# A two-layer hybrid trunk: the last expert in two halves of its inner columns, and the end of the last layer in another form

## The reference

```python
w = aff[top 2 experts of the best group]; w = w / sum(w)
for e in range(16):
    gate, up = split(tok @ w_gu[e])            # 1024 -> 2 x 512
    out = out + comb[:, e:e+1] * ((silu(gate) * up) @ w_down[e])   # 512 -> 1024
x = layer_norm(ALPHA * x + g2 * out, ln_g[l, 1], ln_b[l, 1])
```

## Time and profile before

| | |
|---|---|
| Time, median of 3 runs | 1354.54 us (1351.35 to 1356.68) |
| The profiled execution's own time | 1352.85 us |
| Its span | 1351.0 us |
| Mean granted TensorE clock | 0.966 |
| PE / DVE / ACT / POOL busy | 1244.5 / 1038.0 / 769.2 / 276.5 us |

### The profile page before, as it was taken

The page is one execution under the profiler, slowest core; times in us unless marked ns, Lnnn a source line. Parts: engine busy times, 40 slices in busy tenths (PEclk is TensorE's granted clock), DMA queues, the critical chain, the costliest instruction groups (busy, mean ns, idle before and its releaser), DMA issues.

```text
span 1351.0 us, 17986 instructions
## 1 busy us (share of the span) xinstructions
PE 1244.5 (92%) x6571; PEld 964.2 (71%) x6572; DVE 1038.0 (77%) x1162; ACT 769.2 (57%) x1032; POOL 276.5 (20%) x321
## 2 busy tenths in 40 slices
PE   4999999699999999899998999999959999999975
PEld 4876677477777777569866777857747777777752
DVE  6787768789999998667737666643778999989857
ACT  3523224377777777554635565575347777777750
POOL 0112222100000000337005555444120000000020
PEclk9999999699999999899988999999969999999988
DMA  9887973599999999914943333215359999999961
GB/s 356 304 276 282 339 269 110 205 365 406 392 373 408 386 400 374 371 36 155 234 122 94 110 98 106 94 64 195 127 195 365 385 402 386 391 392 393 373 240 62
DMA packets 111950, 359.22 MB, mean 266 GB/s; under 512 B 8048, under 2 KB 16476, under 8 KB 111850
## 3 DMA queue, kind: packets, MB, share of 16 engines
q1 hardware_dynamic: 89992, 282.10, 57.1%
q0 software_dynamic: 17296, 60.38, 12.5%
q10 hardware_dynamic: 4594, 15.84, 2.9%
HBM read 329.94 MB, written 25.21 MB: 263 GB/s over the span
## 4 chain that ended last, share of the span: by engine, by line
PE 53%; DVE 15%; issue 11%; ACT 10%; DMA 5%; POOL 3%; SPq 1%; ACTq 1%; DVEq 0%; POOLq 0%
PE bank L237 13%; PE bank L238 12%; PE bank L239 12%; ACT w_hi L1399 4%; DMA ada<-in_ada_w_dram 3%; PE bank L2298 2%; DVE acc L468 2%; PE bank L2280 2%; POOL prob L2520 2%; DVE hh L1501 2%; ACT xe_hi L1345 2%; PE bank L1438 2%; PE bank L1328 1%; PE bank L2268 1%; DVE w_lo L232 1%
## 5 line engine op out<-in xcount | busy, mean ns | idle before, releaser
L1405 DVE TENSOR_TENSOR w_lo<-raw,w_hi 128x2048 fp32r<-128x2048 f32 x189 | 433.6, 2298 | 51.8 <-ACT w_hi L1399 49.8
L1399 ACT ACTIVATE w_hi<-raw 128x2048 fp32r<-128x2048 f32 x189 | 362.6, 1918 | 80.7 <-PE bank L239 78.4
L237 PE MATMUL bank<-w_lo,xe_hi 128*128 128x512 f32 x512 | 212.3, 415 | 1.3 <-DVE xe_lo L1360 1.1
L238 PE MATMUL bank<-w_hi,xe_lo 128*128 128x512 f32 x512 | 204.4, 399 | 0.0
L239 PE MATMUL bank<-w_hi,xe_hi 128*128 128x512 f32 x512 | 204.1, 399 | 0.0
L227 ACT ACTIVATE w_hi<-raw 128x2048 fp32r<-128x2048 f32 x37 | 70.6, 1910 | 112.5 <-PE bank L239 84.4
L1317 POOL DMA_INDIRECT xg<-scratch_u,tok x32 | 31.4, 980 | 481.9 <-PE bank L1328 456.8
L237 PE MATMUL bank<-u_lo,w_hi 128*128 128x512 f32 x288 | 119.3, 414 | 9.0 <-DVE q L2185 4.2
L2520 POOL TENSOR_SCALAR prob<-prob,rsum,gates 128x512 f32<-128x512 f32 (+3 forms) x128 | 108.2, 858 | 91.0 <-DVE rsum L2488 91.0
L237 PEld LDWEIGHTS bank<-w_lo,xe_hi 128*128 128x128 f32 x512 | 97.5, 190 | 30.7 <-issue 8.5
L238 PE MATMUL bank<-u_hi,w_lo 128*128 128x512 f32 x288 | 115.6, 401 | 0.0
(11 more groups left out here) (332 smaller groups left out, 2279.9 us busy)
## 6 DMA issues: line engine op xcount, KB each, us to landing
raw<-in_w_gu_dram SPq DMA_DIRECT2D x128, 1024.0 KB, 7.4
raw<-in_w_down_dram SPq DMA_DIRECT2D x64, 1024.0 KB, 6.5
ada<-in_ada_w_dram POOLq DMA_DIRECT2D x48, 512.0 KB, 6.6
ada<-in_ada_w_dram SPq DMA_DIRECT2D x32, 512.0 KB, 3.8
scratch_y<-ye ACTq DMA_DIRECT2D x30, 512.0 KB, 7.2
raw<-in_conv_w_in_dram SPq DMA_DIRECT2D x12, 1024.0 KB, 14.3
mod_w<-in_ada_w_dram SPq DMA_DIRECT2D x8, 1024.0 KB, 14.0
raw<-in_w_kv_dram SPq DMA_DIRECT2D x6, 1024.0 KB, 6.8
```

What stands on the lines that cost most here:

```text
L237: nc.tensor.matmul(o, lh, rl, start=start, stop=False)
L238: nc.tensor.matmul(o, ll, rh, start=False, stop=False)
L1399: nc.scalar.activation(w_hi[:, hslot, :], raw[:, slot, :], ACT.Copy).then_inc(hi_done, 1)
L1405: nc.vector.tensor_tensor(w_lo[:, slot, :], raw[:, slot, :], w_hi[:, hslot, :].bitcast(F32), ALU.subtract).then_inc(lo_done, 1)
```

## The change

The last expert of both layers is computed in two halves of its 512 inner columns. `gate_up_halves` reads the weight block as two strips of 256 columns (gate and up of one half) and fills bank 2 + f with both, for the last two gate and up blocks and for the two that run under expert 14; sg, hh, the transposes (banks 6 and 7), ht_hi and ht_lo come once per half. On VectorE the lo part of the last down block moves behind ht_lo. The silu of the first half waits for a semaphore from the first half of the last gate and up block, the second for the whole block.

In layer 1 ScalarE scales the first gathered row of each tile by its weight, VectorE adds the second one with its weight and multiplies by the gate row (`far_gate_dve`), and VectorE also makes ye, with the gate row in it. `end_pe` sums ALPHA * xt (through a diagonal matrix), the gathered sum (through the identity) and the last expert's part in two banks per tile, other banks for each tile. `norm_end_dve` takes statistics and the first half of the normalization straight from PSUM. For tiles 0 to 2 ScalarE scales and GpSimd adds row 1; for tile 3 VectorE does both in one operation, behind a wait for tile 2. The diagonal matrices are one in place of eight. Left out of the diff: semaphore counts for these steps, and two waits inside the branch that is skipped.

```diff
-    def norm_last_dve(dve, s, i):
-
-        if i == 0:
-            dve.wait_ge(*moes[s.l].pre_in.at(16 * 12))
+    def norm_end_dve(dve, s, i, banks):
+        for h in range(2):
+            nc.vector.bn_stats(ln_stat[:, i, 6 * h:6 * h + 6], bank[banks[h]][:]).then_inc(dve_step, 1)
+            dve_n[0] += 1
+        dve.wait_ge(dve_step, dve_n[0])
+        nc.vector.bn_aggr(ln_mv[:, i, 0:2], ln_stat[:, i, :].rearrange("p (a b) -> p a b", b=6)
+                          ).then_inc(s.stat.sem, 1)
         dve.wait_ge(*s.stat.at(i + 1))
-        nc.vector.scalar_tensor_tensor(out=xt[:, i, :], in0=xt[:, i, :], scalar=ln_mv[:, i, 0:1],
-                                       in1=end_row(0), op0=ALU.subtract, op1=ALU.mult).then_inc(s.gain.sem, 1)
+        for h in range(2):
+            c_ = slice(h * BANK, (h + 1) * BANK)
+            m = nc.vector.scalar_tensor_tensor(out=xt[:, i, c_], in0=bank[banks[h]][:], scalar=ln_mv[:, i, 0:1],
+                                               in1=end_row(0)[:, c_], op0=ALU.subtract, op1=ALU.mult)
+        m.then_inc(s.gain.sem, 1)
         dve.wait_ge(*s.root.at(i + 1))
         nc.vector.reciprocal(ln_mv[:, i, 3:4], ln_mv[:, i, 2:3]).then_inc(s.coef.sem, 1)
-        dve.wait_ge(*s.gain.at(i + 1))
-        dve.wait_ge(*s.coef.at(i + 1))
-        nc.vector.scalar_tensor_tensor(out=xt[:, i, :], in0=xt[:, i, :], scalar=ln_mv[:, i, 3:4],
-                                       in1=end_row(1), op0=ALU.mult, op1=ALU.add).then_inc(s.done.sem, 1)
+        if i == TT - 1:
+            dve.wait_ge(*s.gain.at(i + 1))
+            dve.wait_ge(*s.coef.at(i + 1))
+            dve.wait_ge(*s.done.at(i))
+            nc.vector.scalar_tensor_tensor(out=xt[:, i, :], in0=xt[:, i, :], scalar=ln_mv[:, i, 3:4],
+                                           in1=end_row(1), op0=ALU.mult, op1=ALU.add).then_inc(s.done.sem, 1)
...
+    def norm_scale_act(act, s, i):
+        act.wait_ge(*s.gain.at(i + 1))
+        act.wait_ge(*s.coef.at(i + 1))
+        nc.scalar.activation(xt[:, i, :], xt[:, i, :], ACT.Copy, scale=ln_mv[:, i, 3:4]).then_inc(s.norm.sem, 1)
+    def norm_shift_pool(pool, s, i):
+        pool.wait_ge(*s.norm.at(i + 1))
+        nc.gpsimd.tensor_tensor(xt[:, i, :], xt[:, i, :], end_row(1), ALU.add).then_inc(s.done.sem, 1)
...
+    def half_cols(ap, f):
+        return ap.rearrange("p (h f n) -> p f h n", h=2, f=2)[:, f, :, :]
+    def gate_up_halves(pe, s, pair, p, i, j, last_block=False):
+        b, slot, _, hslot = step_block(s, pair, p, i)
+        pe.wait_ge(lo_done, b + 1)
+        for f in range(2):
+            for kk in range(2):
+                k = 2 * j + kk
+                c_ = slice(kk * D, (kk + 1) * D)
+                m = mm3(bank[2 + f][:].rearrange("p (h n) -> p h n", h=2), xe_hi[:, 1, k, :], xe_lo[:, 1, k, :],
+                        half_cols(w_hi[:, hslot, c_], f), half_cols(w_lo[:, slot, c_], f), start=(k == 0),
+                        stop=(k == KD - 1))
+            if last_block and f == 0:
+                m.then_inc(s.xg_turned.sem, 1)
+        m.then_inc(blk_used, 1)
...
+        ahead_of_last = isinstance(pair, int) and e == NE - 2
+        if last:
+            gate_up_halves(pe, s, pair, p, 0, 2)
+            gate_up_halves(pe, s, pair, p, 1, 3, last_block=True)
+        else:
+            gate_up(pe, s, pair, p, 0, p, 2)
             rows_pe(pe, s, pair + p, q)
-        gate_up(pe, s, pair, p, 1, p, 3)
-        if not last:
+            gate_up(pe, s, pair, p, 1, p, 3)
             pe.wait_ge(*s.xe_lo_made.at(e + 2))
             after(pe, s.h_made, e)
-            gate_up(pe, s, pair, p, 2, q, 0)
+            if ahead_of_last:
+                gate_up_halves(pe, s, pair, p, 2, 0)
+            else:
+                gate_up(pe, s, pair, p, 2, q, 0)
...
         for k in range(4):
-            m = nc.tensor.transpose(bank[6][:, k * P:(k + 1) * P], hh[:, k * P:(k + 1) * P], ident[:])
+            if last and k == 2:
+                m.then_inc(s.h_turned.sem, 1)
+                pe.wait_ge(*s.h_made.at(e + 2))
+            m = nc.tensor.transpose(bank[6 + (k // 2 if last else 0)][:, k * P:(k + 1) * P],
+                                    hh[:, k * P:(k + 1) * P], ident[:])
         m.then_inc(s.h_turned.sem, 1)
-        if not last:
+        if ahead_of_last:
+            gate_up_halves(pe, s, pair, p, 3, 1)
+        elif not last:
             gate_up(pe, s, pair, p, 3, q, 1)
...
+            if last and j == 1:
+                pe.wait_ge(*s.ht_lo_made.at(e + 2))
...
-        act.wait_ge(blk_used, s.b0 + EBLK * e + 4)
-        after(act, s.h_made, e)
-        nc.scalar.activation(sg[:], bank[2 * p][:], ACT.Silu).then_inc(s.sg_made.sem, 1)
-        if not last:
+        if last:
+            act.wait_ge(*s.h_made.at(e))
+            for f in range(2):
+                if f == 0:
+                    act.wait_ge(*s.xg_turned.at(NE + 1))
+                else:
+                    act.wait_ge(blk_used, s.b0 + EBLK * e + 4)
+                nc.scalar.activation(sg[:, f * HALF:(f + 1) * HALF], bank[2 + f][:, 0:HALF], ACT.Silu
+                                     ).then_inc(s.sg_made.sem, 1)
+            for f in range(2):
+                act.wait_ge(*s.h_turned.at(e + f + 1))
+                nc.scalar.activation(ht_hi[:, 2 * f:2 * f + 2, :], bank[6 + f][:, f * HALF:(f + 1) * HALF]
+                                     .rearrange("p (k t) -> p k t", k=2), ACT.Copy).then_inc(s.ht_hi_made.sem, 1)
+        else:
+            act.wait_ge(blk_used, s.b0 + EBLK * e + 4)
+            after(act, s.h_made, e)
+            nc.scalar.activation(sg[:], bank[2 * p][:], ACT.Silu).then_inc(s.sg_made.sem, 1)
             step_hi(act, s, pair, p, 4)
-        act.wait_ge(*s.h_turned.at(e + 1))
...
+            if s.l == 1:
+                m = nc.scalar.activation(dg[:, 0, :], ident[:], ACT.Copy, scale=ALPHA)
+            for j in range(2 * TT if s.l == 0 else 0):
                 m = nc.scalar.activation(dg[:, j, :], ident[:], ACT.Copy, scale=w_far[:, j % 2, j // 2:j // 2 + 1])
...
+        if last and s.l == 1:
+            for i in range(TT):
+                act.wait_ge(*s.yg_in[i].at(32))
+                nc.scalar.activation(yg[2 * i][:], yg[2 * i][:], ACT.Copy, scale=w_far[:, 0, i:i + 1]
+                                     ).then_inc(s.far_scaled.sem, 1)
+            return
...
-        step_lo(dve, s, pair, p, 3)
-        dve.wait_ge(*s.sg_made.at(e + 1))
-        after(dve, s.h_turned, e)
-        nc.vector.tensor_tensor(hh[:], sg[:], bank[2 * p + 1][:], ALU.mult).then_inc(s.h_made.sem, 1)
-        if not last:
+        if last:
+            dve.wait_ge(*s.h_turned.at(e))
+            for f in range(2):
+                c_ = slice(f * HALF, (f + 1) * HALF)
+                dve.wait_ge(*s.sg_made.at(e + f + 1))
+                nc.vector.tensor_tensor(hh[:, c_], sg[:, c_], bank[2 + f][:, HALF:FF], ALU.mult
+                                        ).then_inc(s.h_made.sem, 1)
+            for f in range(2):
+                dve.wait_ge(*s.ht_hi_made.at(e + f + 1))
+                nc.vector.tensor_tensor(ht_lo[:, 2 * f:2 * f + 2, :], bank[6 + f][:, f * HALF:(f + 1) * HALF]
+                                        .rearrange("p (k t) -> p k t", k=2),
+                                        ht_hi[:, 2 * f:2 * f + 2, :].bitcast(F32), ALU.subtract
+                                        ).then_inc(s.ht_lo_made.sem, 1)
+            step_lo(dve, s, pair, p, 3)
+        else:
+            step_lo(dve, s, pair, p, 3)
+            dve.wait_ge(*s.sg_made.at(e + 1))
+            after(dve, s.h_turned, e)
+            nc.vector.tensor_tensor(hh[:], sg[:], bank[2 * p + 1][:], ALU.mult).then_inc(s.h_made.sem, 1)
             step_lo(dve, s, pair, p, 4)
-        dve.wait_ge(*s.ht_hi_made.at(e + 1))
...
+        else:
+            for i in range(TT - 1):
+                norm_shift_pool(pool, s.ln, i)
...
+            if s.l == 1 and i < TT - 1:
+                norm_scale_act(act, s.ln, i)
...
+        if s.l == 1:
+            far_gate_dve(dve, s, 0)
+            dve.wait_ge(blk_used, s.b0 + EBLK * NE)
+            after(dve, s.y_out[1], 16 * (PAIRS - 1))
+            for h in range(2):
+                c_ = slice(h * BANK, (h + 1) * BANK)
+                m = nc.vector.tensor_tensor(ye[:, 1, c_], bank[4 + h][:], row(s.ln.gate)[:, c_], ALU.mult)
+            m.then_inc(s.y_made.sem, 1)
+            for i in range(1, TT):
+                far_gate_dve(dve, s, i)
         over_dve(dve, s)
+        if s.l == 1:
+            for i in range(TT):
+                dve.wait_ge(*s.comb.at(i + 1))
+                norm_end_dve(dve, s.ln, i, END_BANKS[i])
+                if i == TT - 1:
...
+    END_BANKS = ((0, 1), (2, 3), (6, 7), (4, 5))
+    def far_gate_dve(dve, s, i):
+        if i == 0:
+            wait_row(dve, s.ln.gate)
+        dve.wait_ge(*s.far_scaled.at(i + 1))
+        far = yg[2 * i]
```

(56 more changed lines are left out.)

12 lines of the change are left out of this document (7 added, 5 removed).

## The result

| | before | changed |
|---|---|---|
| Median of 5 runs | 1353.28 us (1351.35 to 1356.68) | 1343.65 us (1341.32 to 1345.97) |
| Ratio | | 0.9934 [0.9917, 0.9951], so -8.9 us |
| Profiled execution / its span | 1352.85 / 1351.0 us | 1345.97 / 1344.2 us |
| Mean granted clock | 0.966 | 0.968 |

The kernel became faster by 0.5 to 0.8%, inside the range of the prediction, but by 8.9 us and not by 13.3. The profile taken is that of the slowest of the five changed runs, 6.8 us shorter in its span. The chain of waits, with which the earlier trace rows began, breaks off after three pieces in this trace, so I read the stretches from the timelines.

A forecast was written before the change was run, and what follows sets the result against it. TensorE holds 53% of the chain of waits, but VectorE bounds layer 1's end. Layer 1's 11.3 us plus layer 0's 2.0 make 13.3, taking the 1354.54 us median to 1341; range 1334.5 to 1347.

The forecast's parts named there:

- The halves and the clock: Last expert, layer 1: down starts 2.4 us earlier and full clock saves 1.6 us, together 4.0 us.
- rival (c): Gate and up products fed slower in strips of 256; at half rate 9 us slower, 1363; chance 0.04.
- (d): Last expert's halves do not overlap, handovers cost what they save; only 7.3 us gained, 1347; chance 0.08.
- Layer 1's end: VectorE finishes 4.5 us behind TensorE instead of 11.8; with the earlier down products, 11.3 us gained.
- with it the 3.2 us at a clock of 0.52: Layer 1's combination: the low-clock stretch after TensorE's 3.10 us pause stays as long as before.
- an earlier tile 0: Layer 0's combination starts 2.0 us sooner, limited by the second gather; bounds 4.2 gained to 1 lost.
- the hold-up: Layer 0: w_lo runs over the first gather, so the second lands near 563.4; without it 4.2 us gained.
- a loss of 1: Layer 0's lower bound: block loads starting some 5 us sooner push the gathers, losing 1 us.
- The tail: From VectorE's last operation, 1348.00, to the span's end, 1351.0, brought by the last output transfer; no change in the sum.
- (a): Layer 1's end is paced by VectorE or gathers, late gathers held 2 to 4 us; near 1344; chance 0.22.
- (b): Layer 0 gives nothing and the low clock stays in the down products; 9.7 us gained, 1345; chance 0.16.

The follow-up runs named there:

- e3: Changed kernel with layer 0's last expert whole as before, halves only in layer 1; ratio to before 0.9933.
- e6: Changed kernel with VectorE doing the last operation of all four tiles, without ScalarE's scaling and GpSimd's sums there; ratio to before 0.9954.
- e8: Changed kernel with GpSimd adding the row for tiles 0 and 1 only, VectorE ending tiles 2 and 3; ratio to before 0.9926.
- e10: e6 plus a GpSimd memset of one unread column after VectorE's last operation; one run, no ratio, span 1346.0 us.
- e4: Changed kernel with SyncE issuing layer 0's next two weight loads only after tile 1's gathers have landed; ratio to before 0.9956.
- e11: e9 without VectorE's wait in layer 0 for tile 1's gathered rows; ratio to before 0.9912, median 1339.8 us.
- again: The changed kernel itself, unaltered, timed and profiled a second time; ratio to before 0.9913.
- e2: Changed kernel without halves in either layer, keeping only the new end of layer 1; ratio to before 0.9956.
- e5: e4 with VectorE's next two w_lo in layer 0 also waiting for tile 1's gathers; ratio to before 0.9953.
- e7: Changed kernel with unread TensorE products added: two in layer 1 ahead of the skip, five in layer 0 behind it; ratio to before 0.9963.
- e9: Changed kernel with e5's waits, e8's two tiles, and unread products ahead of the skip (three in layer 0, two in layer 1); ratio to before 0.9914.

## Why the prediction was right, and where not

**The halves and the clock: right.** Down starts 2.83 us earlier (forecast 2.4) and takes 5.88 us at clock 1.00 in all kernels with halves (forecast 5.7); in layer 1 TensorE gained 4.24, forecast 4.0. Gate and up products in strips are still 0.23 us apart, so rival (c) falls; the handovers overlap, so (d) falls.

**Layer 1's end: right in kind, 1.0 us too much.** From TensorE's last product to VectorE's last operation are 4.46 us, forecast 4.52. The GpSimd sum takes 2.34 us, forecast 2.3, though it runs beside VectorE's statistics. The whole stretch gave 10.3 of 11.3. What lacks is the step "with it the 3.2 us at a clock of 0.52": tile 0 ran 6 us at 0.50. In e3 to e6 and e8 the stretch is 37.6 to 37.9, a gain of 11.5 to 11.8. Both profiles of the changed kernel have the long low clock (tile 0 done at 19.1), and the six others with halves, the new end and nothing added in the pause (e3 to e6, e8, e10) the short one (17.6 to 17.9). The expectation of the second profile called this chance; whether it goes with the build is not shown.

**Layer 0: the step that failed.** I took 2.0 us for an earlier tile 0, and the layer lost 1.7. The step named both mechanisms, but costed the hold-up alone and left the loads as a bound ("a loss of 1"). The hold-up was as said: the gather took 2.17 us under a w_lo and the second was issued at 557.82. In the Trainium skill, page GPSIMD Engine Reference, section Key points, GpSimd and VectorE contend when VectorE reads two SBUF inputs; the 2.17, and the 2.75 of 559.06 against 0.94 alone, agree with it. The landing, costed at the 5.3 of the earlier trace rows, took 8.2 with the loads in flight, and e4 shows it at 5.7 with these two held back. That is 2.7 us of the miss at tile 3. With the loads held, 0.9 of the 2.0 is there; the rest went to the low clock behind the longer pause, for tile 0 took 6.9 us there (11.3 to 18.3) and 5.4 before. In e11, which also fills that pause, it takes 5.4 (11.1 to 16.6), and the layer gains 2.7 against before.

**The tail: not in the sum at all.** I let the last transfer follow VectorE's last operation in 3 us, as before. The transfer did so (2.6 us to landing in both), but the program did not end with it. From the end of GpSimd's last operation to the span's end are:

| kernel | GpSimd's last operation ends | span | between |
|---|---|---|---|
| changed / again | 1336.54 / 1338.92 | 1344.2 / 1346.6 | 7.66 / 7.68 |
| e2 / e3 | 1334.86 / 1335.80 | 1342.5 / 1343.5 | 7.64 / 7.70 |
| e4 / e5 | 1332.54 / 1333.63 | 1340.2 / 1341.3 | 7.66 / 7.67 |
| e7 / e10 | 1337.00 / 1338.35 | 1344.7 / 1346.0 | 7.70 / 7.65 |
| e8 / e9 / e11 | 1336.03 / 1334.20 / 1332.17 | 1345.7 / 1343.0 / 1341.0 | 9.67 / 8.80 / 8.83 |

In the first eight the tail is 4.8 to 7.8 us, in the last three, where GpSimd stopped earlier, 3.0 to 3.1. The sum for tile 2 so cost 1.8 us at the end.

**The sum put right:** 10.3 - 1.7 - 1.8 = 6.8, the difference of the two spans with the 0.4 of each sign beside it. The timed gain is 8.9 us (7 to 11 by its interval), and 11.8 when the kernel was timed again (8 to 15).

A slip in the range changes nothing here: its lower bound, 1334.5, is worked out from the profiled execution's 1352.85; from the median it is 1336.

**The rivals.** (a) gave 1344, the nearest number, but not by its mechanism: the last gather landed 7.0 us after issue and held tiles 0 and 1, yet tiles 2 and 3 wait 2.10 us each for TensorE. (b) is half true: layer 0 gave nothing, while the low clock left the down products and, in layer 0, moved to tile 0. In the Trainium skill, page Runtime: NRT & Kernel Launch, section Instruction fetch mechanics, a taken branch stalls when its target lies outside the instructions already fetched; the pauses of 2.94 in layer 1 agree, but the same skip in layer 0 took 0.50 before and 3.35 in e7, so no single price holds.

**Open:** why the stretches' gains of e4 to e11 do not show in times. Medians of 6 to 10 runs carry about 3 us here. Each build has one profile (the changed kernel two), and the two long stretches that the edits leave alone differ by 5.3 and 5.7 us between profiles, more than most of the gains; whether the stretches differ from run to run, or the rest of the program gives the gain back, these runs do not tell.

## What to carry to other kernels

When a step is moved earlier, list what its end releases: here two weight loads left 5 us sooner and met the gathers for which the engine then waited. Weigh what help from another engine buys against what it costs: here it bought 0.3 to 0.9 us on VectorE and cost 1.8 at the program's end. Look at when the helper does its last operation. A sum of stretches from one profile is finer than the times can confirm; below 0.5% say which of the two a claim rests on.
